# One scan of a two-direction RWKV block: the small matmuls of TensorE are issued by one direction, and by one half of the heads, at a time

## The chip, the cores and the metric

The kernel runs on one core of a Trainium2 chip. Its time is the device time of one execution in microseconds. A core has TensorE (matmuls, with a weight load ahead of each), VectorE, ScalarE, GpSimd, a queue for DMAs (SyncE) and 16 DMA engines. They run on their own and wait for each other by semaphores.

## The reference

Two blocks follow each other: a first one of two layers (an RWKV-7 layer and a latent-attention layer) and a second one (differential attention, an RG-LRU and a feed-forward part). The change lies in the recurrence of the RWKV layer alone. For each of 8 heads of width 64, for each of 1280 tokens (256 of context, then 1024 latent) and for both directions:

```python
def rwkv7_scan(r, decay, k, v, a_vec, b_vec, s0, reverse):
    def step(S, inp):
        r_t, w_t, k_t, v_t, a_t, b_t = inp
        sa = jnp.einsum('bhij,bhj->bhi', S, a_t)
        S = S * w_t[:, :, None, :] + sa[..., None] * b_t[:, :, None, :] + v_t[..., None] * k_t[:, :, None, :]
        return S, jnp.einsum('bhij,bhj->bhi', S, r_t)
    xs = tuple(jnp.moveaxis(t, 1, 0) for t in (r, decay, k, v, a_vec, b_vec))
    S, ys = lax.scan(step, s0, xs, reverse=reverse)
    return jnp.moveaxis(ys, 0, 1), S
```

The outputs of both directions are added, go through a group norm, a gate and an output product, and the rest of the two blocks follows. All of it is fp32.

## The kernel before, in words

The kernel is a row of phases, each with a program for every engine and a barrier at its end. The change is in the phase `phase_scan` (L663), and there in TensorE's program only.

The scan works in its chunked form. The 1280 tokens are 10 chunks of 128 (`NB = 10`), each of two halves of 64 tokens (`CH = 64`, index `e` below). Both directions (`d`) are worked on together: direction 1 takes the chunks from the other end, and its halves in the other order (`ORDER`). The 8 heads lie as 4 pairs (`p`) by two halves of the partitions (`h`). Almost every matmul is 64x64: its operands lie in one half of the partitions (the row half of the array), and its output in one half of the partitions of a PSUM bank (the column half). So the array has four quarters, and the quarter of a matmul follows from its slices `half(..)`.

There are eight PSUM banks: `bA`, `bB`, `bC`, `bD`, one of each for a direction. For a chunk `n` the steps are, in TensorE's order (they are mixed with those of the chunk before, which is one chunk behind with its state):

- `gram(n, 0)` and `gram(n, 1)`: products of `bk` and `ar` of a chunk; output by `h` to `bA` or `bB`; 32 matmuls with 128 columns each. VectorE masks them to `sc_mB` (x = 0) and `sc_mK` (x = 1), by `h` and then by `d`.
- `turn_v`, `turn_bk` (L773, L783): full-array transposes; `mask_v` (L794): 32 matmuls of 64 columns on two diagonal quarters.
- `level_p(n, l)` and `level_z(n, l)` (L808, L820), four levels: the inverse of a triangular matrix by blocks, 32 matmuls of 32 columns each, on the two diagonal quarters; between them VectorE makes `sc_Pm`, `sc_Z` and `sc_X`. `last_p`, `last_z` (L831, L843) are its last step, in 32x32 tiles.
- For the chunk before, and for each half `e`: `state_w` (L861, 16 matmuls; VectorE then adds to `sc_W`), `state_u` (L874, 16; ScalarE copies to `sc_U`), `state_ys` (L892, 64; L897, 16), after which VectorE makes the new state and the output `sc_y`.

The main loop (`for n in range(NB + 1)`) sets TensorE's order by hand: gram(n, 0), state_w(n-1, 0), gram(n, 1), state_u(n-1, 0), turn_v, turn_bk(0), state_ys(n-1, 0), turn_bk(1), mask_v, level_p(0), state_w(n-1, 1), level_z(0), level_p(1), state_u(n-1, 1), level_z(1), level_p(2), state_ys(n-1, 1), level_z(2), level_p(3), level_z(3), last_p, last_z. `done(eng, x, d, n, r)` is a wait for the semaphore of step x and direction d, and `settle()` a no-op behind waits. In gram both directions follow each other, and h alternates inside; in the three state steps both directions are waited for first, and then alternate matmul by matmul.

Of the kernel before, what the change touches and what calls it, by code (L numbers as in the profile page):

```python
# [662 lines left out]
def phase_scan(g):  # L663
# [29 lines left out]
    with ExitStack() as ctx:  # L693
# [14 lines left out]
        with nc.Block() as block:  # L708
# [35 lines left out]
            def _(pe):  # L744
# [6 lines left out]
                def gram(n, x):  # L751
                    for d in range(2):
                        if x == 0:
                            pe.wait_ge(ld[d, n % 2], 48 * (n // 2 + 1))
                            if n:
                                done(pe, "Pev", d, n - 1)
                                done(pe, "zf", d, n - 1)
                        else:
                            done(pe, "mB", d, n)
                        settle()  # L760
                        for p in range(4):
                            for q in range(2):
                                for h in range(2):
                                    r, c = half(h), half(q)
                                    last = mm((bA, bB)[h][d][c, 128 * p:128 * p + 128], bk[r, n % 2, d, p, x, c], ar[r, n % 3, d, p, :, c],
                                              start=True, stop=True)
                        last.then_inc(S[("gB", "gK")[x], d], 2)
# [79 lines left out]
                def state_w(n, e):  # L847
                    if n or e:
                        m, f = (n, 0) if e else (n - 1, 1)
                        for d in range(2):  # L850
# [3 lines left out]
                    else:  # L854
                        pe.wait_ge(zeroed, 1)
                    settle()
                    for p in range(4):
                        for h in range(2):
                            for d in range(2):
                                o, c = 256 * h + 64 * p, half(ORDER[d][e])  # L860
                                last = mm((bC, bD)[h][d][c, o:o + 64], ar[half(h), n % 3, d, p, 0, c], St[half(h), d, p], start=True, stop=True)  # L861
                                if p == 3 and h == 1:
                                    last.then_inc(S["W", d], 1)

                def state_u(n, e):
                    for d in range(2):
                        done(pe, "Wev", d, n, 2 * e + 1)
                        if e == 0:
                            done(pe, "zf", d, n)
                    settle()  # L870
                    for j in range(8):
                        for d in range(2):
                            o, c = slice(64 * j, 64 * j + 64), half(ORDER[d][e])
                            last = mm(bC[d][c, o], Zf[c, n % 2, d, j], W[c, d, o], start=True, stop=True)  # L874
                            if j == 7:
# [2427 lines left out]
```

## Time and profile before

| | us |
|---|---|
| median of 3 runs | 3687.27 |
| lowest, highest | 3679.78, 3688.47 |
| profiled execution | 3688.47 |
| its span | 3686.7 |
| the scan, about | 660 to 1180 us of the span |

How to read the rows below. PE is TensorE's matmuls, PEld its weight loads, DVE VectorE, ACT ScalarE, POOL GpSimd. An fp32 matmul leaves two records. A row of a stretch (`A:B length, ...`) has the busy time of each engine with its records in brackets, then the granted TensorE clock (1.00 is 2.4 GHz, 0.50 is 1.2 GHz), the DMA share and GB/s; with a line number in its caption, it counts that line's instructions alone, first the matmuls and then the weight loads. A row of waits has who waited for whom, the sum in us, how often, and the longest. A row of the timeline has the start in us, the length in us, the engine, the line, the operation, its output and inputs, the tile of the array, the shape, and how many records are merged; in brackets the idle time before it.

### The profile page before, as it was taken

The numbers are of one execution on the slowest core, as the hardware profiler recorded it, in microseconds if no ns is written. First come the engines' busy times: TensorE is split into PE (matmuls) and PEld (weight loads), VectorE is DVE, ScalarE is ACT, GpSimd is POOL, SyncE is SP. The second block draws the span as 40 slices with busy tenths as digits, with TensorE's granted clock in tenths as the row PEclk, the third lists the DMA queues.
The fourth block names the chain that finished last, engine by engine and source line by source line (L and its number), as shares of the span: only waits on it lengthen the run. The fifth ranks groups of instructions, "written<-read, shape, count | busy, mean of one in ns | idle before, by whom it ended". The sixth has DMA issues, their size and how long they took to land. (4 is left out here: it accounts for less than half of the span.)

```text
span 3686.7 us, 62343 instructions
## 1 busy us (share of the span) xinstructions
PE 3296.3 (89%) x27450; PEld 2755.4 (75%) x27450; DVE 1805.7 (49%) x2463; ACT 1178.6 (32%) x1648; POOL 393.9 (11%) x272
## 2 busy tenths in 40 slices
PE   5599999798986689897999989998777999999999
PEld 3488888688886479855899977776546788888887
DVE  6454455455653542253555534753443463636364
ACT  0444334222222322255444422542552211111111
POOL 0122221000000112110000012211102000000000
PEclk9799999778876899999999999999788999999999
DMA  8112231422212321324112013122002111111112
GB/s 346 43 70 101 105 125 72 122 72 72 72 43 94 131 92 46 117 85 173 57 59 63 31 61 126 47 78 94 29 18 86 52 40 57 42 56 43 54 45 76
DMA packets 145995, 294.53 MB, mean 80 GB/s; under 512 B 10048, under 2 KB 86976, under 8 KB 140224
## 3 DMA queue, kind: packets, MB, share of 16 engines
q1 hardware_dynamic: 126608, 212.95, 17.1%
q0 software_dynamic: 19120, 77.60, 6.2%
q8 instruction: 218, 3.57, 0.4%
q14 instruction: 49, 0.40, 0.0%
HBM read 211.22 MB, written 79.30 MB: 79 GB/s over the span
## 5 line engine op out<-in xcount | busy, mean ns | idle before, releaser
L60 PE MATMUL ev_ps<-h_hi,ev_w_hi 128*128 128x512 f32 (+1 forms) x792 | 288.5, 364 | 36.5 <-POOL ev_w_lo L360 35.2
L60 PE MATMUL ff_ps<-h_hi,ff_w_hi 128*128 128x512 f32 x768 | 300.1, 391 | 2.2 <-DVE ff_w_lo L3043 2.2
L61 PE MATMUL ff_ps<-h_lo,ff_w_hi 128*128 128x512 f32 x768 | 299.8, 390 | 0.0
L62 PE MATMUL ff_ps<-h_hi,ff_w_lo 128*128 128x512 f32 x768 | 299.7, 390 | 0.0
L62 PE MATMUL ev_ps<-h_hi,ev_w_lo 128*128 128x512 f32 (+1 forms) x792 | 281.1, 355 | 0.0
L61 PE MATMUL ev_ps<-h_lo,ev_w_hi 128*128 128x512 f32 (+1 forms) x792 | 281.1, 355 | 0.0
L3043 DVE TENSOR_TENSOR ff_w_lo<-ff_w,ff_w_hi 128x1024 fp32r<-128x1024 f32 (+1 forms) x80 | 89.5, 1119 | 339.5 <-ACT ff_w_hi L3018 339.5
L60 PEld LDWEIGHTS ev_ps<-h_hi,ev_w_hi 128*128 128x128 f32 x792 | 150.5, 190 | 75.1 <-POOL ev_w_lo L360 36.0
L3018 ACT ACTIVATE ff_w_hi<-ff_w 128x1024 fp32r<-128x1024 f32 (+1 forms) x80 | 78.0, 975 | 326.3 <-PE ff_ps L62 324.0
L60 PEld LDWEIGHTS ff_ps<-h_hi,ff_w_hi 128*128 128x128 f32 x768 | 144.8, 189 | 34.0 <-DVE ff_w_lo L3043 3.8
L62 PEld LDWEIGHTS ff_ps<-h_hi,ff_w_lo 128*128 128x128 f32 x768 | 144.8, 189 | 30.3
L61 PEld LDWEIGHTS ff_ps<-h_lo,ff_w_hi 128*128 128x128 f32 x768 | 144.9, 189 | 30.1
L61 PEld LDWEIGHTS ev_ps<-h_lo,ev_w_hi 128*128 128x128 f32 x792 | 150.6, 190 | 21.7 <-issue 1.7
L62 PEld LDWEIGHTS ev_ps<-h_hi,ev_w_lo 128*128 128x128 f32 x792 | 150.4, 190 | 21.2
L2861 ACT ACTIVATE ma_e<-ma_s,ma_nm 128x1280 f32<-128x1280 f32 x64 | 84.9, 1327 | 217.7 <-DVE ma_nm L2895 217.7
L2835 PE MATMUL ma_o<-ma_pt,ma_v 128*128 128x128 f32 x1280 | 153.2, 275 | 0.0
L60 PE MATMUL ff_ps<-ff_mid_hi,ff_w_hi 128*128 128x512 f32 x384 | 149.4, 389 | 0.0
L61 PE MATMUL ff_ps<-ff_mid_lo,ff_w_hi 128*128 128x512 f32 x384 | 149.4, 389 | 0.0
L62 PE MATMUL ff_ps<-ff_mid_hi,ff_w_lo 128*128 128x512 f32 x384 | 149.4, 389 | 0.0
L2835 PEld LDWEIGHTS ma_o<-ma_pt,ma_v 128*128 128x128 f32 x1280 | 147.9, 192 | 0.0
L360 POOL TENSOR_TENSOR ev_w_lo<-ev_w,ev_w_hi 128x1024 fp32r<-128x1024 f32 x33 | 92.3, 2798 | 367.1 <-ACT ev_w_hi L432 367.1
L3074 DVE SCALAR_TENSOR_TENSOR ff_acc<-ff_rows,cols,ff_acc 128x1023 f32<-128x1023 f32 x96 | 123.2, 1284 | 3.4
(501 smaller groups left out, 8065.7 us busy)
## 6 DMA issues: line engine op xcount, KB each, us to landing
ff_w<-in_w_up SPq DMA_DIRECT2D x48, 512.0 KB, 3.5
ev_w<-in_ev_w_in POOLq DMA_DIRECT2D x33, 512.0 KB, 3.9
ada_wt<-in_ada_w POOLq DMA_DIRECT2D x12, 1024.0 KB, 8.5
ada_wt<-in_ada_w SPq DMA_DIRECT2D x12, 1024.0 KB, 8.7
ff_w<-in_w_down SPq DMA_DIRECT2D x32, 384.0 KB, 3.0
ar<-ev_ar SPq DMA_DIRECT2D x8, 1280.0 KB, 5.4
bk<-ev_bk SPq DMA_DIRECT2D x8, 1280.0 KB, 8.0
sc_ar<-ar SPq DMA_DIRECT2D x20, 512.0 KB, 6.1
```

The costliest lines, as they stand in the source:

```text
L60: nc.tensor.matmul(out, w_hi, x_hi, start=start, stop=False)
L61: nc.tensor.matmul(out, w_hi, x_lo, start=False, stop=False)
L62: return nc.tensor.matmul(out, w_lo, x_hi, start=False, stop=stop)
L360: nc.gpsimd.tensor_tensor(w_lo[:, n % 2], w[:], w_hi[:, n % 2].bitcast(F32), ALU.subtract).then_inc(w_lo_done, 1)
L2835: mm = nc.tensor.matmul(po[:, u % 2, 0:P], v[:, h % 2, t], pt[:, u % 2, t * P:t * P + P], start=t == 0, stop=t == NT - 1)
L2861: nc.scalar.activation(e[:, s % 2], ps[:, 0:T], ACT.Exp, bias=nm[:, s % 2:s % 2 + 1], accum_out=sm[:, s % 2:s % 2 + 1]).then_inc(exps, 1)
L3018: nc.scalar.activation(w_hi[:, n % 2, 0:kt(n)], w[:, n % 2, 0:kt(n)], ACT.Copy).then_inc(w_hi_done, 1)
L3043: nc.vector.tensor_tensor(w_lo[:, n % 2, 0:kt(n)], w[:, n % 2, 0:kt(n)], w_hi[:, n % 2, 0:kt(n)].bitcast(F32), ALU.subtract).then_inc(w_lo ...
L3074: nc.vector.scalar_tensor_tensor(out=acc[:, x, i:LAT], in0=rows[:, 0:LAT - i], scalar=tap[2 - i], in1=acc[:, x, i:LAT], op0=ALU.mult, op1= ...
```

## The change

`gram` gets the head half `h` as an argument and is called for h = 0 and then for h = 1: all matmuls of `bA` of both directions, then all of `bB`. For x = 0 the wait for the chunk's loads stays with h = 0, the wait for `Pev` (bank A is free) goes with h = 0 and the wait for `zf` (bank B is free) with h = 1; for x = 1 each h waits for its own `mB`. The semaphores `gB` and `gK` rise by one a half and not by two at the end. In `state_w`, `state_u` and `state_ys` the loop over d is outermost: wait, no-op, matmuls and semaphore of direction 0, then those of direction 1. No matmul is added or left out, and the programs of the other engines stay as they are.

```diff
@@ -748,23 +748,22 @@
 
                     pe.nop(nofuse=True)
 
-                def gram(n, x):
-                    for d in range(2):
+                def gram(n, x, h):
+                    for d in range(2):
+                        out = (bA, bB)[h][d]
                         if x == 0:
-                            pe.wait_ge(ld[d, n % 2], 48 * (n // 2 + 1))
+                            if h == 0:
+                                pe.wait_ge(ld[d, n % 2], 48 * (n // 2 + 1))
                             if n:
-                                done(pe, "Pev", d, n - 1)
-                                done(pe, "zf", d, n - 1)
+                                done(pe, ("Pev", "zf")[h], d, n - 1)
                         else:
-                            done(pe, "mB", d, n)
+                            done(pe, "mB", d, n, h)
                         settle()
                         for p in range(4):
                             for q in range(2):
-                                for h in range(2):
-                                    r, c = half(h), half(q)
-                                    last = mm((bA, bB)[h][d][c, 128 * p:128 * p + 128], bk[r, n % 2, d, p, x, c], ar[r, n % 3, d, p, :, c],
-                                              start=True, stop=True)
-                        last.then_inc(S[("gB", "gK")[x], d], 2)
+                                r, c = half(h), half(q)
+                                last = mm(out[c, 128 * p:128 * p + 128], bk[r, n % 2, d, p, x, c], ar[r, n % 3, d, p, :, c], start=True, stop=True)
+                        last.then_inc(S[("gB", "gK")[x], d], 1)
 
                 def turn_v(n):
                     for d in range(2):
@@ -845,68 +844,65 @@
                         last.then_inc(S["lastZ", d], 1)
 
                 def state_w(n, e):
-                    if n or e:
-                        m, f = (n, 0) if e else (n - 1, 1)
-                        for d in range(2):
+                    for d in range(2):
+                        c = half(ORDER[d][e])
+                        if n or e:
+                            m, f = (n, 0) if e else (n - 1, 1)
                             done(pe, "snew", d, m, f)
                             done(pe, "y1", d, m, f)
                             done(pe, "y", d, m, f)
-                    else:
-                        pe.wait_ge(zeroed, 1)
-                    settle()
-                    for p in range(4):
-                        for h in range(2):
-                            for d in range(2):
-                                o, c = 256 * h + 64 * p, half(ORDER[d][e])
+                        else:
+                            pe.wait_ge(zeroed, 1)
+                        settle()
+                        for p in range(4):
+                            for h in range(2):
+                                o = 256 * h + 64 * p
                                 last = mm((bC, bD)[h][d][c, o:o + 64], ar[half(h), n % 3, d, p, 0, c], St[half(h), d, p], start=True, stop=True)
-                                if p == 3 and h == 1:
-                                    last.then_inc(S["W", d], 1)
+                        last.then_inc(S["W", d], 1)
 
                 def state_u(n, e):
                     for d in range(2):
+                        c = half(ORDER[d][e])
                         done(pe, "Wev", d, n, 2 * e + 1)
                         if e == 0:
                             done(pe, "zf", d, n)
-                    settle()
-                    for j in range(8):
-                        for d in range(2):
-                            o, c = slice(64 * j, 64 * j + 64), half(ORDER[d][e])
+                        settle()
+                        for j in range(8):
+                            o = slice(64 * j, 64 * j + 64)
                             last = mm(bC[d][c, o], Zf[c, n % 2, d, j], W[c, d, o], start=True, stop=True)
-                            if j == 7:
-                                last.then_inc(S["U", d], 1)
+                        last.then_inc(S["U", d], 1)
 
                 def state_ys(n, e):
-                    b = n % 2
-                    for d in range(2):
+                    for d in range(2):
+                        c, b = half(ORDER[d][e]), n % 2
                         done(pe, "Uev", d, n, e)
-                    settle()
-                    for p in range(4):
-                        for x in (2, 3, 0, 1):
-                            for h in range(2):
-                                for d in range(2):
-                                    c, r, j = half(ORDER[d][e]), half(h), 4 * h + p
+                        settle()
+                        for p in range(4):
+                            for x in (2, 3, 0, 1):
+                                for h in range(2):
+                                    r, j = half(h), 4 * h + p
                                     o, ov = half(j), half(2 * p + h)
                                     at = 64 * p + (256 if x >= 2 else 0)
                                     lhs, rhs = ((U[c, d, o], mB[c, b, d, j, 1]), (V[c, b, d, ov], mK[c, b, d, j, 1]),
                                                 (Bt[c, b, d, 0, ov], U[c, d, o]), (Bt[c, b, d, 1, ov], V[c, b, d, ov]))[x]
                                     mm(bD[d][r, at:at + 64], lhs, rhs, start=x % 2 == 0, stop=x % 2 == 1)
-                    for p in range(4):
-                        for h in range(2):
-                            for d in range(2):
-                                c, r = half(ORDER[d][e]), half(h)
+                        for p in range(4):
+                            for h in range(2):
+                                r = half(h)
                                 last = mm(bC[d][r, 64 * p:64 * p + 64], St[r, d, p], ar[r, n % 3, d, p, 1, c], start=True, stop=True)
-                                if p == 3 and h == 1:
-                                    last.then_inc(S["YS", d], 1)
+                        last.then_inc(S["YS", d], 1)
 
                 pe.wait_ge(consts, 96)
                 for n in range(NB + 1):
                     new, old = n < NB, n >= 1
                     if new:
-                        gram(n, 0)
+                        gram(n, 0, 0)
+                        gram(n, 0, 1)
                     if old:
                         state_w(n - 1, 0)
                     if new:
-                        gram(n, 1)
+                        gram(n, 1, 0)
+                        gram(n, 1, 1)
                     if old:
                         state_u(n - 1, 0)
                     if new:
```

Three places show how the rows of TensorE's program move. In the names, `sc_bA0` is bank A of direction 0. A row with x8 is eight equal matmuls in a row.

At the end of a chunk and the start of the next, before the change, TensorE (last_z, then gram(n, 0), direction 0 first):

```order
L843 MATMUL sc_bB0<-sc_Z,sc_P5 32x32 x16
L843 MATMUL sc_bB1<-sc_Z,sc_P5 32x32 x16
L765 MATMUL sc_bA0<-sc_ar,sc_bk 64x128
L765 MATMUL sc_bB0<-sc_ar,sc_bk 64x128
L765 MATMUL sc_bA0<-sc_ar,sc_bk 64x128
L765 MATMUL sc_bB0<-sc_ar,sc_bk 64x128
L765 MATMUL sc_bA0<-sc_ar,sc_bk 64x128
L765 MATMUL sc_bB0<-sc_ar,sc_bk 64x128
```

The same place in the changed program, TensorE:

```order
L842 MATMUL sc_bB0<-sc_Z,sc_P5 32x32 x16
L842 MATMUL sc_bB1<-sc_Z,sc_P5 32x32 x16
L765 MATMUL sc_bA0<-sc_ar,sc_bk 64x128 x8
L765 MATMUL sc_bA1<-sc_ar,sc_bk 64x128 x8
L765 MATMUL sc_bB0<-sc_ar,sc_bk 64x128 x8
L765 MATMUL sc_bB1<-sc_ar,sc_bk 64x128 x8
```

Banks A and B no longer alternate: each has its eight matmuls of a direction in a row, and all of bank A stands ahead of bank B.

After gram(n, 1), before the change, TensorE (the end of gram and the start of state_u):

```order
L765 MATMUL sc_bA1<-sc_ar,sc_bk 64x128
L765 MATMUL sc_bB1<-sc_ar,sc_bk 64x128
L874 MATMUL sc_bC0<-sc_W,sc_Zf 64x64
L874 MATMUL sc_bC1<-sc_W,sc_Zf 64x64
L874 MATMUL sc_bC0<-sc_W,sc_Zf 64x64
L874 MATMUL sc_bC1<-sc_W,sc_Zf 64x64
L874 MATMUL sc_bC0<-sc_W,sc_Zf 64x64
L874 MATMUL sc_bC1<-sc_W,sc_Zf 64x64
```

The same place in the changed program, TensorE, up to the start of state_ys:

```order
L872 MATMUL sc_bC0<-sc_W,sc_Zf 64x64 x8
L872 MATMUL sc_bC1<-sc_W,sc_Zf 64x64 x8
L772 MATMUL sc_bA0<-ident_sb,sc_vt 128x128 x4
L772 MATMUL sc_bA1<-ident_sb,sc_vt 128x128 x4
L782 MATMUL sc_bB0<-ident_sb,sc_bk 128x128 x4
L782 MATMUL sc_bB1<-ident_sb,sc_bk 128x128 x4
L888 MATMUL sc_bD0<-sc_U,sc_Bt 64x64 x2
L888 MATMUL sc_bD0<-sc_V,sc_Bt 64x64 x2
L888 MATMUL sc_bD0<-sc_mB,sc_U 64x64 x2
L888 MATMUL sc_bD0<-sc_mK,sc_V 64x64 x2
```

state_u has the eight matmuls of direction 0 in a row and then those of direction 1, and state_ys begins with direction 0 alone. Before the change state_ys, TensorE, began like this:

```order
L892 MATMUL sc_bD0<-sc_U,sc_Bt 64x64
L892 MATMUL sc_bD1<-sc_U,sc_Bt 64x64
L892 MATMUL sc_bD0<-sc_U,sc_Bt 64x64
L892 MATMUL sc_bD1<-sc_U,sc_Bt 64x64
L892 MATMUL sc_bD0<-sc_V,sc_Bt 64x64
L892 MATMUL sc_bD1<-sc_V,sc_Bt 64x64
```

There the directions alternated, and two matmuls of a direction in a row are its two head halves.

## Rows read from the trace of the kernel before

**Rows 1.** The page, its first line:

```profile
span 3686.7 us, 62343 instructions
```

**Rows 2.** Stretches, all engines: the scan, and two of nine periods.

```profile
660.00:1180.00 520.00, 446.39 (x13040) 428.55 (x13040) 285.22 (x623) 122.11 (x261) 26.07 (x22) 0.78 0.25 65
...
714.70:761.42 46.72, 43.90 (x1304) 42.62 (x1305) 28.27 (x62) 12.08 (x26) 2.50 (x2) 0.79 0.16 43
...
1098.82:1145.00 46.18, 42.88 (x1232) 41.57 (x1234) 27.39 (x61) 11.73 (x25) 2.51 (x2) 0.80 0.05 15
```

**Rows 3.** Waits of TensorE in the scan, 660 to 1180 us:

```profile
PE sc_bA L808 <- DVE sc_X L988: 12.5, 22, 0.9
PE sc_bA L765 <- DVE sc_mB L959: 7.6, 9, 1.5
PE sc_bC L897 <- issue: 4.1, 4, 1.2
...
PE sc_bD L892 <- ACT sc_U L1073: 2.6, 2, 1.3
PE sc_bC L861 <- DVE sc_y L1028: 2.3, 1, 2.3
...
PE sc_bC L874 <- DVE sc_W L1012: 1.7, 1, 1.7
```

**Rows 4.** Timeline of TensorE in gram at clock 0.50:

```profile
1100.13 0.42 PE L765 MATMUL sc_bA<-sc_ar,sc_bk 64*64 64x128 f32 x1
1100.16 0.42 PE L765 MATMUL sc_bB<-sc_ar,sc_bk 64*64 64x128 f32 x1
1100.17 0.42 PE L765 MATMUL sc_bA<-sc_ar,sc_bk 64*64 64x128 f32 x1
1100.18 0.42 PE L765 MATMUL sc_bB<-sc_ar,sc_bk 64*64 64x128 f32 x1
1100.34 0.42 PE L765 MATMUL sc_bA<-sc_ar,sc_bk 64*64 64x128 f32 x1
```

**Rows 5.** Stretches, L765 alone: a gram(n, 0) and a gram(n, 1).

```profile
1098.80:1102.50 3.70, 3.68 (x64) 3.31 (x64) 0.50 0.00 0
912.80:914.90 2.10, 1.98 (x64) 1.76 (x64) 1.00 0.00 0
```

**Rows 6.** Stretch, L861 alone (state_w, e = 0).

```profile
815.00:816.20 1.20, 1.08 (x32) 0.99 (x32) 0.50 0.00 1
```

**Rows 7.** Stretches, L874 alone: state_u, e = 0 and e = 1.

```profile
914.90:916.20 1.30, 1.15 (x32) 1.04 (x32) 1.00 0.00 0
...
884.50:886.60 2.10, 1.99 (x32) 1.81 (x32) 0.51 0.03 8
```

**Rows 8.** Stretches, L892 alone: e = 0, the last chunk, and e = 1.

```profile
724.40:726.70 2.30, 2.10 (x128) 1.96 (x128) 1.00 0.00 0
...
1166.70:1170.50 3.80, 3.69 (x128) 3.53 (x128) 0.50 0.02 4
...
843.90:847.60 3.70, 3.62 (x128) 3.51 (x128) 0.58 0.02 4
```

**Rows 9.** Stretch, L897 alone, e = 1.

```profile
847.40:848.60 1.20, 1.15 (x32) 1.03 (x32) 1.00 0.00 0
```

**Rows 10.** Timeline of TensorE at the seam of level_p(0) and state_w.

```profile
879.00 0.27 PE L861 MATMUL sc_bC<-sc_S,sc_ar 64*64 64x64 f32 x1
879.04 0.28 PE L808 MATMUL sc_bA<-sc_X,sc_mD 64*64 64x32 f32 x3
...
879.11 0.22 PE L808 MATMUL sc_bA<-sc_X,sc_mD 64*64 64x32 f32 x1
...
879.16 0.22 PE L808 MATMUL sc_bA<-sc_X,sc_mD 64*64 64x32 f32 x1
...
879.17 0.22 PE L808 MATMUL sc_bA<-sc_X,sc_mD 64*64 64x32 f32 x1
```

**Rows 11.** Stretch, L820 alone: level_z(1).

```profile
837.45:841.20 3.75, 3.67 (x64) 3.59 (x64) 0.50 0.02 4
```

**Rows 12.** Stretch, L808 alone: level_p(2).

```profile
840.85:844.40 3.55, 3.51 (x64) 3.55 (x64) 0.50 0.00 0
```

**Rows 13.** Line L874: its weight loads, least, median and longest in ns.

```profile
L874 PEld LDWEIGHTS sc_bC<-sc_W,sc_Zf x640: 129/135/228, 721.5 to 1165.1; 64*64 64x64 f32 x160
```

## The prediction

> **What bounds the kernel now.** I read the page first, then the stretches by engine, then TensorE's own lines in the scan, then the order of a few rounds, then the waits. The page gives a span of 3686.7 us [rows 1]; the profiled execution took 3688.47 us, 1.8 us around the span, and the median of the three runs is 3687.27. The change touches the scan alone, 660 to 1180 us. There TensorE is busy 446.39 of 520 us, VectorE 285.22, ScalarE 122.11 [rows 2]. Between the second start of gram(n, 0) and the place where an eleventh would stand (714.70 and 1145.00, nine periods) lie 430.3 us, 47.8 us a period; the first and the last of them stand in [rows 2], with TensorE busy for 43 to 44 us of 46 to 47. So a TensorE microsecond added is nearly a microsecond added to the end, unless it falls into one of the few idle gaps: before gram(n, 1) 7.6 us in 9 gaps for sc_mB, before the level product (L808) 12.5 us in 22 for sc_X, and in the last chunk 2.6 for sc_U and 2.3 for y [rows 3].
>
> What a matmul costs is to be read in rounds. Each fp32 matmul leaves two records in the trace, so 32 matmuls of gram(n, x) are 64 records. Four records start together, within 50 ns, and the next four 0.21 us later [rows 4]: four 64x64 quarters of the array work at once, because the code alternates h (row half) and q (column half). Hence 16 rounds: 3.68 us at a granted clock of 0.50, 1.98 at 1.00 [rows 5]; without the tail of the last record 3.41 and 1.71, that is 213 and 107 ns a round. The stretches of 64 columns go by 32 records in 8 rounds of four for L861 (1.08 us at 0.50) [rows 6], by 32 records in 16 rounds of two for L874 (1.15 us at 1.00, 1.99 at 0.51) [rows 7], by 128 records in 32 rounds of four for L892 (2.10 at 1.00, 3.69 at 0.50) [rows 8]: 58 ns a round at 1.00, 107 at 0.50. L897 takes 1.15 for 32 records [rows 9], rounds of two.
>
> **The change, part by part.** No matmul is added. What changes is how many quarters have work at a time: in gram four become two (one row half, both columns); in state_w four become two; in state_u two become one, since each direction has one diagonal quarter; in L892 four become two; L897 stays at two, as row and column half go together. What was beside comes after. Per period, with the clock at the level that each stretch has now:
> gram(n, 0), mostly at 0.50: 16 rounds become 32, +3.41. gram(n, 1), at 1.00: +1.71. state_u(n-1, 0) at 1.00: 16 more rounds of 58 ns, +0.93; state_u(n-1, 1), mostly at 0.50: 16 x 0.107 = +1.71. L892 at e = 0: 32 more rounds, +1.88; at e = 1 the clock is at 0.50 and rises within it (0.58 in the mean, 3.62 us [rows 8]); what is added comes behind the rise, +1.88 again. state_w(n-1, 0): 8 more rounds, +0.86, but the 0.85 us (7.6/9 [rows 3]) of waiting for sc_mB goes, since sc_mB of h = 0 is ready while h = 1 is still multiplied: 0. state_w(n-1, 1): +0.47, beside the gap of up to 0.9 us before the next L808, where VectorE sets the start: 0; without that gap it would cost the 0.47. Together 11.5.
>
> Some comes back at the seams. At 879.00 L861 starts its first record while L808 still has 6 to start [rows 10]: where the next group has other quarters, 6 records run beside the old ones. That is 3 rounds of 107 to 213 ns for each gram, 6 of 58 to 107 for each state_u, and some 0.15 for each L892: about 2.2 a period. So 9.3 a period, 84 us for nine.
>
> The waits that are split cost nothing: behind a wait for one direction on TensorE stand that direction's matmuls, and the other's come later than now. VectorE and ScalarE take direction 0 first anyway, so only direction 1's copies see it, and they are not late: sc_U is needed two transposed groups later. The added waits and no-ops (4 a gram pair, 1 a state step) are bounded by the seams in the trace, which show no gap at such a point: 0 to 0.05 us each, up to 0.5 a period; I take 0. "Issue" stalls, 22 us over the scan on TensorE in eight rows of the view (4.1 is the largest [rows 3]), fall into dense stretches; thinner ones may shorten them. Bounds 0 and -15; I take -5.
>
> **The clock** is the large unknown. In a period it stands at 0.50 through both level stretches of 837 to 844 us (3.67 and 3.51 us) [rows 11, 12], through gram(n, 0) [rows 5] and state_w [rows 6]. It rises at two places: during or just before gram(n, 1), and during L892 of e = 1 (0.58), so that L897 is at 1.00 [rows 8, 9]. Ahead of both rises stand stretches in which four quarters work. The long stretches with two quarters at 32 columns stayed at 0.50 [rows 11, 12]. After the change gram and L892 have two quarters in one row half. I forecast that these rises come later in about half the periods: for gram only with the full-array transposes (L773, L783), for L892 not before the next period's. What a late rise costs, by the rows at 0.50 against 1.00: gram(n, 1) 32 x 0.106 less seams = 3.1, state_u(n-1, 0) 1.6, first transposes 1.2: 5.9; and L892 + 1.9, L897 0.8, two levels of 1.6, part of a third 0.6: 6.5. Whole 12.4 a period. Bounds: 0 and 12.4; no row shows a two-quarter stretch of 64 or 128 columns long enough to be nearer one end, so the middle, 6.2.
>
> **Sum.** 9 x (9.3 + 6.2) = 140. First chunk: gram +3.4 and +1.7, less the 1.5 us wait for sc_mB, and a late rise 4.4: +8. Last chunk, where nothing fills in: u and L892 twice at 0.50 add 1.7 + 3.4 each; direction 0 starts about 0.9 + 1.2 earlier each, and the y wait of 2.3 goes: +4. Less 5 for issue. 140 + 8 + 4 - 5 = +147 on 3688.5: 3835 us.
>
> **The Trainium skill** has two rules here, neither used in the sum. "TensorE: Matmul & The Clock Gate", Part 3, says that a weight load overlaps matmuls in flight only where the row group differs. The trace disagrees: in gram two records share each row half, and still 64 fit into 16 rounds [rows 4, 5]. By that rule the change would be dearer (rival 4). The same page gives a 64-deep queue with a reorder window. By it the second direction could be taken beside the first (rival 3); the trace shows 6 records.
>
> **Rivals.**
> 1. The clock rises and falls as now. For it: it may count busy time, and TensorE is no less busy. Against: the level stretches are as busy and stayed at 0.50. 84 + 4 + 4, less 5: +87, 3775.
> 2. All those rises are late. For it: only four-quarter stretches stand ahead of them. Against: transposes use the whole array, and thinner work leaves fewer falls, since the gap before L808 shrinks. 9 x 21.7 + 12 - 5 = +202, 3890.
> 3. Not slower: TensorE takes up free quarters further ahead than a group is long. Then direction 1 or h = 1 runs beside the other as now, and what is left is the removed waits: sc_mB 7.6, sc_U 2.6, y 2.3 and W 1.7 of the last chunk: -14, 3674. It decides from 16 records ahead, the length of a group of gram, w and u. Against it: at 879.00 all that L861 waits for was long done and its quarter was free, and it was still taken up only 6 records early.
> 4. One row half at a time keeps loads from overlapping. The shortest weight load is 129 ns [rows 13]; on 64 + 64 + 128 rounds of gram, u and L892 that is at most 33 us a period, +300, about 4130 with the rest. Against it: L897 is issued with four records in a row for one quarter and still takes 1.15 us.
>
> **How the numbers follow.** Main case 0.50, its own range 3800 to 3870; rival 1 0.20, rival 2 0.21, rival 3 0.04, rival 4 0.05. The range 3770 to 3900 holds the main case and the two clock rivals, with little over at the top; it leaves out rivals 3, 4 and the far edges of rivals 1 and 2. Within 0.3% (11 us, about what a measurement of this kernel can tell from no change) lies only a part of rival 3. Faster 0.03, same 0.02, slower 0.95.
>
> **What would show it.** In the profile after: two gram records per start, 64 of them in about 3.4 us at 1.00 and 6.8 at 0.50; state_u of 32 records near 1.9 or 3.4; L892 of 128 near 3.8 or 6.9; no wait for sc_mB before gram; 47.8 us a period become 61 to 65; L808, L820, L773 unchanged at equal clock; VectorE's sum the same. The clock in the scan tells which case: mean 0.78 now, about 0.70 in the main case, 0.60 in rival 2. It is wrong if four records still start together, if a single quarter takes more than 60 ns a record at 1.00, or if time moves outside 660 to 1180 us.

## The result: slower by 4.3%, and the profile after

| | before | after |
|---|---|---|
| median, us | 3684.82 (4 runs) | 3834.68 (4 runs) |
| lowest, highest | 3679.78, 3688.47 | 3829.46, 3870.79 |
| profiled execution, its span | 3688.47, 3686.7 | 3845.05, 3843.3 |
| ratio to before | | 1.043 [1.0373, 1.0485] |
| scan, first to last TensorE record | 498.8 | 650.6 |

The forecast was 3835 us in 3770 to 3900. The scan grew by 151.8 us of the 156.6 by which the two spans differ. The ratio goes by all six executions of the changed kernel (mean 3843.07 us, two of them not in the median's four). Differences against the changed kernel in single numbers below are of the medians in the table (+150 us), and since its own runs lie 41 us apart they are good to some 20 us.

The page of the kernel after: the span, the busy times, and the TensorE clock in 40 slices, against [rows 1].

```profile
span 3843.3 us, 62413 instructions
...
PE 3489.2 (91%) x27450; PEld 2955.5 (77%) x27450; DVE 1812.8 (47%) x2463; ACT 1183.0 (31%) x1648; POOL 402.8 (10%) x272
...
PEclk8799999666665579999899999999788999999999
```

The slices 8 to 14 are the scan: 6 and 5 tenths of full clock. The same kernel's stretches, all engines: the whole scan, what lies between the second start of gram(n, 0) and the tail of the last period, and two periods, against [rows 2].

```profile
660.00:1340.00 680.00, 636.64 (x13040) 626.73 (x13040) 293.92 (x623) 125.91 (x261) 28.55 (x26) 0.63 0.20 53
...
725.28:1288.90 563.62, 555.02 (x11482) 546.95 (x11480) 256.87 (x545) 111.20 (x232) 22.82 (x18) 0.65 0.17 43
...
725.28:786.77 61.49, 60.73 (x1308) 59.94 (x1305) 29.21 (x62) 12.34 (x26) 2.53 (x2) 0.67 0.15 39
...
1040.49:1101.89 61.40, 60.64 (x1307) 59.86 (x1304) 29.18 (x62) 12.33 (x26) 2.53 (x2) 0.67 0.20 52
```

A period took 46.72 us and takes 61.49. VectorE's work in it went from 28.27 to 29.21, ScalarE's from 12.08 to 12.34; TensorE's went from 43.90 to 60.73, with as many records, and now leaves 0.8 us idle where it left 2.8. The work is the same, it stands one piece behind the other, and the clock is at 0.67 and not 0.79.

The timeline of TensorE after, at a seam inside gram(n, 0), at a clock of 0.50, against [rows 4]; rows of one bank are merged, and the last column counts records.

```profile
789.25 0.84 PE L765 MATMUL sc_bA<-sc_ar,sc_bk 64*64 64x128 f32 x5
789.68 0.48 PE L765 MATMUL sc_bB<-sc_ar,sc_bk 64*64 64x128 f32 x2
789.81 0.50 PE L765 MATMUL sc_bA<-sc_ar,sc_bk 64*64 64x128 f32 x2
789.95 0.42 PE L765 MATMUL sc_bB<-sc_ar,sc_bk 64*64 64x128 f32 x2
```

Inside a bank two records go per 0.21 us (five records in 0.84 us, 0.42 of it the last one's length). Only at the seam, from 789.68 to some 790.3, do the two row halves overlap: bank B has begun while five records of bank A, counted singly, were still to start (the rows shown end before the fifth, at 790.32).

Stretches of the kernel after, each with its own line alone, in this order: L765 (gram) at 0.50 and at 0.97, L860 (state_w), L872 (state_u) at 1.00 and 0.50, L888 (was L892) at 1.00 and 0.50, L807 (was L808), L819 (was L820).

```profile
786.70:793.30 6.60, 6.53 (x64) 6.18 (x64) 0.50 0.61 148
1047.85:1051.20 3.35, 3.35 (x64) 3.16 (x62) 0.97 0.00 0
...
792.50:794.85 2.35, 2.20 (x32) 1.87 (x31) 0.50 0.00 0
...
797.90:799.70 1.80, 1.64 (x32) 1.50 (x29) 1.00 0.00 0
816.40:819.80 3.40, 3.29 (x32) 3.16 (x32) 0.50 0.00 0
...
801.30:805.90 4.60, 4.27 (x128) 3.99 (x128) 1.00 0.02 4
826.20:833.80 7.60, 7.33 (x128) 6.95 (x127) 0.50 0.01 2
...
822.80:826.50 3.70, 3.70 (x64) 3.60 (x64) 0.50 0.02 4
...
841.10:844.90 3.80, 3.69 (x64) 3.56 (x64) 0.50 0.98 264
```

Against [rows 5 to 9, 11, 12]: gram 3.68 became 6.53 at 0.50, state_w 1.08 became 2.20, state_u 1.15 and 1.99 became 1.64 and 3.29, L892 2.10 and 3.69 became 4.27 and 7.33. The levels, which the change does not touch, cost nearly the same at 0.50 (L807 3.70 for 3.51, L819 3.69 for 3.67), but are at 0.50 more often.

Waits of TensorE in the scan after, 660 to 1340 us, against [rows 3]:

```profile
PE sc_bA L765 <- DMA sc_eye<-in_eye: 18.4, 1, 18.4
PE sc_bA L807 <- DVE sc_X L984: 5.8, 9, 0.7
PE sc_bB L819 <- issue: 2.4, 1, 2.4
PE sc_bC L860 <- DVE sc_y L1024: 1.7, 1, 1.7
PE sc_bB L842 <- issue: 1.7, 2, 1.2
PE sc_bC L872 <- DVE sc_W L1008: 0.9, 2, 0.5
```

The wait for sc_mB (7.6 us) is gone and the one for sc_X fell from 12.5 to 5.8; the first row stands ahead of the scan in both.

**Where the 151.8 us are.** From the single records of the two traces I gave each group of matmuls the time from each start to the next, less idle gaps, and noted how much of it lay at clock 0.50 ("cold"). "At full clock" is the time less half the cold part. That is a convention: in the kernel before a level record follows the one ahead of it by 30.6 ns at 1.00 and by 53.8 at 0.50, less than double, so the levels' 151.8 and 143.6 differ though their work does not, and the split between rounds and clock is good to some 10 us. All figures of this kind, here and below, are of one execution of each kernel.

| group | before: us, cold, at full clock | after: us, cold, at full clock | us more |
|---|---|---|---|
| gram | 57.6, 38.9, 38.2 | 100.9, 86.3, 57.8 | 43.3 |
| L892 | 49.2, 20.7, 38.9 | 106.6, 73.6, 69.8 | 57.4 |
| state_u | 26.4, 13.1, 19.8 | 51.5, 40.9, 31.1 | 25.1 |
| state_w | 17.4, 9.6, 12.6 | 23.6, 16.3, 15.4 | 6.2 |
| L897 | 22.2, 1.6, 21.4 | 26.7, 18.3, 17.5 | 4.5 |
| levels | 190.2, 76.8, 151.8 | 234.5, 181.8, 143.6 | 44.3 |
| transposes, mask_v, last | 86.1, 32.0, 70.1 | 94.0, 53.5, 67.3 | 7.9 |
| waits named | 27.7 | 8.5 | -19.2 |
| "issue" | 22.1 | 4.3 | -17.8 |

So the matmuls cost 49.8 us more at full clock, the clock 139.1 more, and 37.0 of idle time went. (The table's L892 and L897 are the old line numbers; the changed kernel has them as L888 and L892.) The clock rose 18 times in the scan before and 10 times after: 6 in gram, 1 in the transposes, 3 in L892 of e = 0, and never in L892 of e = 1.

### The profile page after: what moved, and what is told of

Read it like the earlier page. It is cut to its first block and busy times, and to the rows that moved or that the text cites. A ratio compares the mean times of both kernels' runs of the same rounds, so it can differ in the third digit from the quotient of the medians.

```text
span 3843.3 us, 62413 instructions
## 1 busy us (share of the span) xinstructions
PE 3489.2 (91%) x27450; PEld 2955.5 (77%) x27450; DVE 1812.8 (47%) x2463; ACT 1183.0 (31%) x1648; POOL 402.8 (10%) x272
## 3 DMA queue, kind: packets, MB, share of 16 engines
q1 hardware_dynamic: 126608, 212.95, 16.3%
## 5 line engine op out<-in xcount | busy, mean ns | idle before, releaser
L60 PE MATMUL ev_ps<-h_hi,ev_w_hi 128*128 128x512 f32 (+1 forms) x792 | 289.0, 365 | 40.2 <-POOL ev_w_lo L360 38.9
L61 PEld LDWEIGHTS ev_ps<-h_lo,ev_w_hi 128*128 128x128 f32 x792 | 150.8, 190 | 21.6 <-issue 1.7
L360 POOL TENSOR_TENSOR ev_w_lo<-ev_w,ev_w_hi 128x1024 fp32r<-128x1024 f32 x33 | 100.8, 3053 | 363.7 <-ACT ev_w_hi L432 363.7
L819 PE MATMUL sc_bB<-sc_Z,sc_Pm 64*64 64x32 f32 x2560 | 133.1, 273 | 2.4 <-issue 2.4
```

The costliest lines, as they stand in the source:

```text
L60: nc.tensor.matmul(out, w_hi, x_hi, start=start, stop=False)
L61: nc.tensor.matmul(out, w_hi, x_lo, start=False, stop=False)
L360: nc.gpsimd.tensor_tensor(w_lo[:, n % 2], w[:], w_hi[:, n % 2].bitcast(F32), ALU.subtract).then_inc(w_lo_done, 1)
L819: last = mm(bB[d][c, 32 * j:32 * j + 32], Pm[c, d, j], Z[c, d, j], start=True, stop=True)
```

## The experiments

Each kernel was timed against the kernel before on its own chip: 3687.11 us (19 runs) for gram_split, states_split, gram_by_row and gram_by_column, 3689.65 (13) for more_noops, u_twice, wide_before and wide_after, 3690.49 (13) for the rest. "Before" and "after" are the two kernels above. Two theories: (a) quarters of the array stand idle, because a group of matmuls for other quarters is taken up only a few records ahead; (b) on top of that the clock stays at 0.50 longer. The rivals: the split waits and the added no-ops cost, or any grouping costs, however short.

**gram_split and states_split: the halves of the change.** Each has its part of the diff, the other part stays as before:

```diff
-                        gram(n, 0)                          # gram_split, in gram and its calls
+                        gram(n, 0, 0)
+                        gram(n, 0, 1)
...
-                    for j in range(8):                      # states_split, in state_w, state_u, state_ys
-                        for d in range(2):
+                    for d in range(2):
+                        settle()
+                        for j in range(8):
```

> The kernel before with the change to gram alone (h = 0 of both directions, then h = 1, with the waits split); the state steps alternate as before. Quarters and clock: 32 more rounds a chunk in gram, 16 of them mostly at 0.50, less the 7.6 us of waiting for sc_mB and some of the issue stalls, and the clock rises later before gram(n, 1) in part of the chunks: +30 to +75 us, about +50. Rival, the cost sits in the state steps and their chain of waits: 0 to +10 us here.

Measured 3748.7 us, 1.0165 [1.013, 1.0201].

> The kernel before with the change to state_w, state_u and state_ys alone; gram as before. Quarters and clock: u 16 more rounds and L892 32 more rounds each twice a chunk, and the rise inside L892 of e = 1 is lost while the one at gram(n, 0) and gram(n, 1) stays: +70 to +110 us, about +90; with gram_split it adds up to about the whole +150. Rival, gram is what costs: under +30 us.

Measured 3744.47 us, 1.0148 [1.0117, 1.0179]. By medians the two give +62 and +57, 119 together, where both at once give 150. The states part is below what I expected. In it the levels are cold for 98.0 us, against 76.8 before and 181.8 with both parts; in gram_split they are cold for 68.3, and it is gram (110.9 of 110.9 us) and state_u (36.8 of 38.5) that stay cold, up to the transposes. gram_split's stretch of L772, the first transposes of a chunk, which stood at 1.00 before:

```profile
789.40:791.40 2.00, 1.97 (x8) 1.57 (x8) 0.50 0.00 0
```

So each half alone lengthens the time at 0.50 on its own side of the period only, and both together lengthen it on the level side more than the states half does by itself. states_split is also the changed kernel with gram put back, and lies 90 us below it.

**gram_by_row and gram_by_column: same banks, waits and semaphores as before, another order in gram.**

```diff
-                        for p in range(4):
-                            for q in range(2):
-                                for h in range(2):
+                        for h in range(2):            # gram_by_row
+                            for p in range(4):
+                                for q in range(2):
...
+                        for q in range(2):            # gram_by_column
+                            for p in range(4):
+                                for h in range(2):
```

> The kernel before, in gram only the loop order changed within a direction: h outermost, so the two quarters that work at once lie in one row half; waits and semaphores as before. Quarters and clock: as gram_split plus the wait for sc_mB, so within about 15 us of it, +35 to +80. Rival, it is the splitting of the waits that costs: 0 here.

Measured 3705.63 us, 1.0047 [1.0032, 1.0063]: slower, but by 18.5 us and not the 35 to 80 expected.

> As gram_by_row, but q outermost: the two quarters that work at once lie in one column half and in both row halves. Both have the same number of rounds of two. If the clock goes by how much of the array works, it is the same time as gram_by_row within 10 us. If it goes by how long the rows are fed, whichever columns take it, the clock in gram is as before the change or higher, and it is faster than gram_by_row by 15 to 50 us; then gram(n, 1) stands at 1.00 in nearly all chunks. If a weight load overlaps only with matmuls of the other row half, gram_by_row needs more than 107 ns a round at 1.00 and this one does not.

Measured 3700.2 us, 1.0032 [1.0017, 1.0046]. The stretches of L765, first of gram_by_row, then of gram_by_column, two each:

```profile
770.10:774.40 4.30, 4.23 (x62) 4.26 (x64) 0.50 0.01 4
825.50:828.00 2.50, 2.43 (x64) 2.42 (x64) 1.00 0.02 7
```

```profile
771.00:773.50 2.50, 2.42 (x64) 2.38 (x64) 1.00 0.02 7
818.80:821.40 2.60, 2.56 (x64) 2.47 (x64) 1.00 0.02 6
```

I had left out the seams. With 16 records per run the next run (other quarters) starts early at each of three seams. The timeline of gram_by_row at one:

```profile
770.62 0.88 PE L765 MATMUL sc_bA<-sc_ar,sc_bk 64*64 64x128 f32 x6
771.09 0.48 PE L765 MATMUL sc_bB<-sc_ar,sc_bk 64*64 64x128 f32 x2
771.26 0.45 PE L765 MATMUL sc_bA<-sc_ar,sc_bk 64*64 64x128 f32 x2
771.35 0.42 PE L765 MATMUL sc_bB<-sc_ar,sc_bk 64*64 64x128 f32 x2
```

Bank B begins with six records of A still to start, so much of a short run lies beside its neighbours: 4.23 us, where four at a time take 3.68 and after has 6.53. At equal clock the two orders cost the same (2.43 and 2.42 us a stretch at 1.00, 43.9 and 44.0 us for gram at full clock, 38.2 before), so a weight load does not ask for the other row half. In the two profiled executions gram was cold for 64.2 of 76.0 us by row and for 34.9 of 61.4 by column; five kernels whose gram keeps four quarters at work (before, more_noops, runs_of_two, wide_before, states_split) lie between 38.9 and 41.9. But these two executions are 14.5 us apart (by column's is the fastest of its ten), and the medians only 5.4, within the 10 us that I had named for no difference and below the 15 to 50 for the other case. The intervals against the kernel before overlap. Compared directly, the ten runs of each have means 6.7 us apart, by row is the slower in 82 of the 100 pairs, and the granted clocks of all twenty give by row 18 us more at 0.50 in the mean, where the two profiled executions give 31. So there is a difference of the clock, of about half the size that the two profiles show.

**runs_of_two: quarters change every four records, in gram, state_u and L892.**

```diff
-                            for q in range(2):              # gram
-                                for h in range(2):
+                            for h in range(2):
+                                for q in range(2):
...
-                    for j in range(8):                      # state_u
-                        for d in range(2):
+                    for j, d in ((2 * i + k, d) for i in range(4) for d in range(2) for k in range(2)):
...
-                            for h in range(2):              # L892
-                                for d in range(2):
+                            for d in range(2):
+                                for h in range(2):
```

> The kernel before, but gram, state_u and L892 of state_ys issue two matmuls (four records) of one pair of quarters (one quarter in state_u) and then two of the other, instead of one and one. Theory, TensorE takes up a free quarter up to 6 records ahead: runs of four records hide inside that, so the rounds stay four wide (two in state_u) and the time is that of before within 0.3%. Rival, any grouping by row half or direction costs in proportion to the seams: a third or more of the change's loss, +50 us.

Measured 3693.37 us, 1.001 [0.9997, 1.0024]. Runs of 4 records, below the six of look-ahead, cost nothing that can be measured; in gram runs of 16 cost 0.5% (0.3% by column), and runs of 32 (gram_split) 1.65%. The rival that any grouping costs falls.

**more_noops: before, with the no-op of gram and of the state steps issued twice (100 more).**

```diff
                         settle()
+                        settle()
```

> The kernel before with a second no-op at each place where gram and the state steps have one. Quarters and clock: the no-ops that the change adds are free, within 0.3% of before. Rival, they drain TensorE's queue and cost at the seams: at 0.2 us each some 100 of them would be +20 us.

Measured 3688.04 us, 0.9994 [0.9983, 1.0006]. The no-ops are free. The split waits have no run of their own; in the changed kernel's trace no wait grew and the waits named fell by 19.2 us.

**u_twice: after, with each matmul of state_u issued a second time into the idle column half.** The copies land where nobody reads them.

```diff
+                            mm(bC[d][half(1 - ORDER[d][e]), o], Zf[c, n % 2, d, j], W[c, d, o], start=True, stop=True)
                             last = mm(bC[d][c, o], Zf[c, n % 2, d, j], W[c, d, o], start=True, stop=True)
```

> The changed kernel, in state_u each matmul is issued a second time into the idle column half of the same row half (its result is not used). Quarters: the other quarter is idle, so 32 more matmuls a chunk cost no round: 0 against the changed kernel, within its own spread of about 15 us, and L872's stretch stays near 1.6 us at 1.00 and 3.0 at 0.50. Rival, matmuls of one row half follow each other or the issue sets the pace: state_u doubles, about +40 to +50 us.

Measured 3859.13 us, 1.0438 [1.0401, 1.0476], overlapping after's interval. The timeline, copies (L872) and originals (L873) at 0.50:

```profile
940.39 0.31 PE L872 MATMUL sc_bC<-sc_W,sc_Zf 64*64 64x64 f32 x1
940.40 0.31 PE L873 MATMUL sc_bC<-sc_W,sc_Zf 64*64 64x64 f32 x1
940.50 0.31 PE L872 MATMUL sc_bC<-sc_W,sc_Zf 64*64 64x64 f32 x1
940.50 0.31 PE L873 MATMUL sc_bC<-sc_W,sc_Zf 64*64 64x64 f32 x1
```

Twice the records in the same rounds of 0.11 us: state_u at full clock is 30.7 us against 31.1. So the other column half did stand idle. Filling it did not raise the clock: state_u was cold for 0.97 of its time (0.79 in after) and gram for 0.98 (0.86).

**wide_before and wide_after: each level matmul writes 64 columns, its 32 twice, into the free part of the bank.** VectorE then reads one copy (of the first product it reads both, where it used to read one twice).

```diff
-  mm(bA[d][c, 32 * j:32 * j + 32], mD[c, d, j], X[c, d, j], ...)
+  mm(bA[d][c, 64 * j:64 * j + 64].rearrange("s (a k) -> s a k", a=2), mD[c, d, j],
+     X[c, d, j].unsqueeze(1).broadcast_to([CH, 2, 32]), ...)      # level_z the same, with bB, Pm, Z
```

> The kernel before; the 32 matmuls of each level_p and level_z write 64 columns, each of the 32 twice, so that the rows of the array are fed twice as long with the same number of matmuls; VectorE reads one copy (or both, where it duplicated them itself). Clock theory: a round of L820 stays at 58 ns at 1.00 and 107 at 0.50, as for 64 columns in L794, and the clock stays at 1.00 through the levels: of 212 us at 0.50 in the scan some 130 go, so -50 to -80 us. Rival, the round is set by the columns streamed or the clock does not answer to them: +0 to +100 us.

Measured 3668.98 us, 0.9941 [0.9924, 0.9959]: faster than the kernel before by 20.7 us, less than expected. Stretches of wide_before, L808 (level_p) and L821 (level_z) alone:

```profile
888.80:891.00 2.20, 2.08 (x64) 1.97 (x64) 1.00 0.03 7
...
890.80:893.10 2.30, 2.08 (x64) 1.97 (x64) 1.00 0.86 229
```

The levels are never at 0.50: 162.7 us with none cold, where they took 190.2 with 76.8 cold. From 714.70 to 1145.00, the stretch that holds nine periods in before and somewhat more here, the clock of wide_before is 0.92 (before: 0.81):

```profile
714.70:1145.00 430.30, 361.80 (x11948) 342.94 (x11940) 258.61 (x569) 110.77 (x238) 22.55 (x18) 0.92 0.22 57
```

What I had not counted stands in its waits, against [rows 3]:

```profile
PE sc_bD L894 <- issue: 8.4, 7, 1.4
PE sc_bB L845 <- issue: 7.7, 2, 4.0
PE sc_bA L765 <- DVE sc_mB L961: 7.3, 9, 1.5
PE sc_bB L765 <- issue: 7.2, 3, 3.2
PE sc_bC L899 <- issue: 6.3, 6, 1.5
...
PE sc_bA L765 <- issue: 4.7, 3, 3.1
```

"Issue" went from 22.1 to 44.2 us: TensorE is quicker through its matmuls and then stands in gaps in which it waits for nothing that the profile shows. The matmul groups gave 44 us, the scan got 20.3. Where these gaps come from stays open.

> The changed kernel with the same wide levels. Clock theory: if what the change cost beyond its rounds is the clock, the level stretches come back to 1.00 and carry gram and L892 with them, which then feed one row half the whole time at 1.00: -130 to -200 us against the changed kernel, so near or under the kernel before, 3640 to 3710. Rival, the change's cost is rounds and waits alone: it stays at +80 us or more over wide_before's counterpart, and no more than 60 us come off, 3775 or over.

Measured 3743.13 us, 1.0138 [1.0116, 1.0161]: 91.6 us below after, and not the 130 to 200 expected. The levels are at 161.4 us with none cold (234.5 with 181.8 before), L892 at 83.8 (106.6); gram stays cold (92.8 of 104.2) and issue went from 4.3 to 19.1. What is left against wide_before is 74 us, 82.6 in the two profiled scans: 60.6 more at full clock (the rounds), 61 more of clock (122 us more at 0.50, 53 of it in gram, 25 in the transposes), and 39 less idle.

**after_ys_before and after_u_before: after, with one state step as it was.** The edits put back the old `state_ys`, or the old `state_u`:

```diff
-                    for d in range(2):                      # after_u_before; state_ys alike
-                        settle()
-                        for j in range(8):
+                    settle()
+                    for j in range(8):
+                        for d in range(2):
```

> The changed kernel with state_ys as before. By the changed kernel's trace its stretches and those of L897 lengthened by 62 us, of which some 30 are rounds and the rest clock; with four quarters at e = 1 the rise there comes back and with it part of the levels: -55 to -90 us against the changed kernel, 3745 to 3780. Rival, the clock inside a chunk is lost to gram alone: -30 us only.

Measured 3756.01 us, 1.0187 [1.0157, 1.0216], 78.7 below after, as expected. L892 fell from 106.6 to 46.7 us, and the levels' cold part from 181.8 to 48.2.

> The changed kernel with state_u as before. By the trace its stretches lengthened by 25 us: 11 us of rounds and 14 of clock. The rounds come back, the clock hardly: -10 to -30 us against the changed kernel. Rival, the split waits let direction 0 start early and earn something: 0 or more.

Measured 3761.63 us, 1.0185 [1.0148, 1.0223]: 73 below after, where 10 to 30 were expected, a miss by far. Of it state_u itself is 19.2 us (51.5 to 32.3; at full clock 31.1 to 21.6). The rest is clock: the levels' cold part fell from 181.8 to 62.1, that of L892 from 73.6 to 26.5. Stretches of after_u_before, L872 (state_u, e = 1) and then L819 (level_z(1)), which in after stood at 0.50:

```profile
923.20:924.70 1.50, 1.16 (x32) 1.05 (x32) 1.00 0.05 11
...
924.20:926.50 2.30, 2.04 (x64) 1.98 (x64) 1.00 0.00 0
```

Either step alone brings much of the levels' clock back, so the parts of the change do not add: put back one at a time, gram gives 90, u 73 and ys 79, 242 in all for a loss of 150, while the two halves done alone cost 62 and 57.

**wide_last: wide_before, with last_p and last_z doubled to 64 columns too.** 

```diff
-  mm(bB[d][ra:ra + 32, 32 * j:32 * j + 32], P5[ro:ro + 32, d, j], Z[ro:ro + 32, d, j], ...)
+  mm(bB[d][ra:ra + 32, 64 * j:64 * j + 64].rearrange("s (a k) -> s a k", a=2), P5[ro:ro + 32, d, j],
+     Z[ro:ro + 32, d, j].unsqueeze(1).broadcast_to([32, 2, 32]), ...)      # last_p the same, with bA, mB, X
```

> wide_before with the 32x32 matmuls of last_p and last_z made 64 columns wide as well. In wide_before the clock falls only behind the last stage, and gram(n, 0) still stands at 0.50 in most chunks (40 us at 0.50 in gram). If that fall comes from thin feeding in the last stage, gram(n, 0) is at 1.00 more often and 5 to 20 us come off wide_before. If it comes from the issue stalls of 3 to 4 us there, nothing changes, within 8 us of wide_before (3669).

Measured 3666.57 us, 0.9942 [0.9922, 0.9962]: the same as wide_before. gram's cold part fell from 40.1 to 26 us and "issue" from 44.2 to 32.6, but last_p and last_z took 40.7 us and not 29.6.

## Why the prediction was right, and which sizes were not

**Rounds and quarters: right.** Two gram records start together where four did, 64 of them in 6.53 us at 0.50 and 3.35 at 0.97 (6.8 and 3.4 forecast). state_u was forecast at 1.9 and 3.4, and took 1.64 (with the seam) and 3.29; L892 at 3.8 and 6.9, and took 4.27 and 7.33. The look-ahead was five or six records at 19 of the 20 seams between bank A and bank B in the changed kernel, and six at all 20 in gram_split. u_twice shows the free quarter directly. Rival 3 (look-ahead as deep as a group) fell with that: 4 records in a row are free (runs_of_two), 16 are not (gram_by_row).

The rounds term was too large all the same. Each group at its new full-clock time and its old share of cold gives gram +29.6, L892 +39.1, state_u +15.1, state_w +3.9, L897 -4.0: 84 us, or 76 with the sc_mB wait (7.6) that I set against state_w. The same term of the prediction is 103.5 for nine periods less 19.8 for seams, 5.1 less 1.5 for the first chunk, 10.2 less 4.2 for the last: 93. By stretch and at full clock, state_u grew by 0.57 us (11.3/20), where 0.93 less 0.35 of seam was forecast; L892 by 1.55 (30.9/20) for 1.88 less 0.15; gram by 0.98 (19.6/20) for 1.71 less 0.32. The step of the prediction that failed here is what "comes back at the seams": gram has a seam inside, between bank A and bank B, beside the one at its end, and I had counted one. With 3 rounds of 107 ns at each of two seams 1.71 less 0.64 is 1.07, near the 0.98 measured.

**Waits: right in kind, larger.** The sc_mB wait went, no gap appeared at a new no-op, and more_noops prices the no-ops at nothing. But the sc_X, sc_U, y and W waits fell by 10.7 us together, of which I had counted 2.3. "Issue" fell by 17.8, where I took 5, and even past the -15 that I had as the far end: the mis-sized term of that step. wide_before shows the other direction (+22.1 us when the work gets shorter).

**The clock: mechanism right, size too small.** I took half of 12.4 us a period, on the ground that the rises on both sides would be late in about half the periods. Keeping each group's old share of cold in the sum above, what is left is clock, and for groups that the change does not touch the whole difference is: L892 18.3, L897 8.5, levels 44.3, last_p and last_z 1.7, 73 on the level side; gram 13.7, state_u 10.0, state_w 2.3, transposes 6.5, 32 on the gram side. That is 105 us, where the prediction has 9 x 6.2 + 4.4 = 60. On the level side the rise in L892 of e = 1 was gone in every period, and it was dearer than the 6.5 that I gave it (8.1); the gram side mostly rose in gram, so it lost 3.6 of its 5.9. The mean clock is 0.63 in the stretch around the scan (0.78 before) and 0.67 in the two periods shown, where 0.70 was forecast for the main case and 0.60 for rival 2: the clock came out between the two. This is the term that was off most, 60 us for a measured 105.

**The sum.** Prediction: 93 for rounds, -2 other waits, -5 issue, +60 clock, 146. Measured: 76, -12, -18, +105, 151. The time of 3835 us was hit because the clock's error of 45 met 40 of the other sign in three terms. The forecast was added to the profiled execution, and between the two profiled executions lie 156.6 us, between the medians 149.9. The range and its reason (both ends of the clock) are what the profile supported; the exact figure is luck. Rival 1 (clock as now) is refuted by after's 476.6 us at 0.50 against 211.5. Rival 2 was right for one side of the period, and the same thinner idle time that I held against it did show up, as fewer falls of the clock within the scan: 10 for 17.

**Rival 4, the weight loads.** After, the two records that start together share a row half, and so do those behind them, at 0.21 us a pair, no dearer than a round of four, and the rival at 4130 us fell. The Trainium skill, "TensorE: Matmul & The Clock Gate", Part 3 (The mechanism), lets a weight load overlap matmuls in flight only across row groups. This trace disagrees: in state_u at 816.40 one quarter works at a time, and the weight loads are busy for 3.16 us of the 3.29 of the matmuls. The same section of the Trainium skill has matmuls start strictly in program order. The seam above disagrees too: bank B's record at 789.68 starts ahead of bank A's at 789.81, which stands before it in the program.

**What is shown and what is not.** Shown by undoing and by doing alone: that idle quarters and the clock make up the loss, that the no-ops have no part, and that the parts of the change interact. That the split waits cost nothing is read from the trace alone, and state_w was neither changed nor put back by itself. Not settled: why the clock is at 0.50 for longer where one row half works at a time. It was so in gram_by_row against gram_by_column, in u_twice and in after against after_u_before, but no run varied the row half with all else equal, and which property of the work the clock follows was not shown.

**A version that beats both:** wide_before, 0.9941 [0.9924, 0.9959] of the kernel before.

## What to carry to other kernels

Here the small fp32 matmuls had to alternate between quarters of the array every few records: four records in a row for the same quarters were free, sixteen were not, and between these nothing was tried. A reordering that looks like pure bookkeeping ("one direction first") was a change of how many quarters work. Price the clock for the whole period at once, because stretches that the edit does not touch (here the levels, +44 us) can pay a third of the bill. Parts undone one by one can add up to more than the whole (here 242 for 150), and parts done alone to less (119). When a stretch is short on columns and the bank has room, try writing the same columns twice before reordering anything, and look at the "issue" rows to see how much of the gain comes through.

## What the runs showed of the hardware that I had not expected

- A 64x64 quarter took 64 columns at 1.00 in nearly the time of 32: a level record followed the one ahead of it by 31.8 ns with 64 columns (wide_before) and by 30.6 with 32 (the records of before at 1.00), and the wide ones never fell to 0.50 where the narrow ones spent 76.8 us there.
- Of two orders of gram with equal rounds, the one with one row half at a time was cold for 64.2 us in its profiled execution, the one with both row halves for 34.9.
- One state step of 16 matmuls (state_u, twice a chunk), put back to both row halves at a time, took 120 us of cold time away from the levels next to it.
- Filling an idle column half with copies did not raise the clock: state_u's cold share went from 0.79 to 0.97.
- A quicker TensorE ran into "issue" gaps of up to 4.0 us each, 44.2 us in the scan for 22.1.
